# Three reorderings in a two-layer decoder step: merged tiles rounded one by one, the first pair of a normalised stage, and gated splits behind masks

## What is computed

```python
h = rmsnorm(x, norm1_g) * (1.0 + sc1) + sh1
z = h @ w_in                                   # q | k | v | g | xl | gl | ma | mb, 8192 columns
q = rope(q); k = rope(k) * DK_RET ** -0.5
o, s_ret_new = retention(q, k, v, s_ret)       # per-head decay, chunks of 128; then a norm per head
p_ret = (o * silu(g)) @ w_proj_ret
p_lru = rg_lru_block(xl, gl, ...) @ w_proj_lru
m = sigmoid(ma) * p_ret + sigmoid(mb) * p_lru
x = x + gt1 * (m @ w_out)
h2 = rmsnorm(x, norm2_g) * (1.0 + sc2) + sh2
x = x + gt2 * (square(relu(h2 @ w_mlp1)) @ w_mlp2)
```

## Time and profile before

| | |
|---|---|
| median of 3 runs | 2120.17 us (2119.0 to 2121.91) |
| the profiled execution, its own time | 2128.43 us |
| its span, first to last instruction | 2126.6 us |
| mean granted clock of TensorE | 0.988 |
| PE busy | 2071.5 us, 97% |
| DVE, ACT, POOL busy | 50%, 34%, 11% |
| DMA | 232.68 MB, mean 109 GB/s |

### The profile page before, as it was taken

How to read it: one execution, slowest core, us unless ns; L and a number is a source line. 1 busy time by engine, 2 the same in 40 slices (tenths; PEclk the granted TensorE clock), 3 DMA queues, 4 the chain that set the end, 5 groups by cost and what they waited for, 6 DMA issues and landing times.

```text
span 2126.6 us, 36627 instructions
## 1 busy us (share of the span) xinstructions
PE 2071.5 (97%) x15244; PEld 1985.4 (93%) x15244; DVE 1072.9 (50%) x1691; ACT 726.6 (34%) x931; POOL 231.8 (11%) x238
## 2 busy tenths in 40 slices
PE   6999999999999999999999999999999999999997
PEld 3899989999998999999989998899999899999997
DVE  4535556675345444444455355667734453535353
ACT  3124434665233222222231244446632321212122
POOL 0001020000032000000220011100000410101014
PEclk8999999999999999999999999999999999999998
DMA  8542243222243333333332313422222422222222
GB/s 344 188 147 86 76 159 99 80 77 82 87 151 109 119 114 120 114 120 119 119 139 80 99 56 125 139 85 78 78 90 71 157 70 82 88 80 81 87 81 100
DMA packets 78924, 232.68 MB, mean 109 GB/s; under 512 B 7360, under 2 KB 27840, under 8 KB 78528
## 3 DMA queue, kind: packets, MB, share of 16 engines
q1 hardware_dynamic: 56304, 204.86, 28.1%
q10 hardware_dynamic: 22480, 25.78, 3.8%
HBM read 218.52 MB, written 12.09 MB: 108 GB/s over the span
## 4 chain that ended last, share of the span: by engine, by line
PE 96%; DVE 2%; DMA 1%; ACT 1%; issue 1%; SPq 0%; DVEq 0%
PE acc L1205 85%; PE acc L1256 2%; PE misc L1277 2%; PE misc L1437 1%; DMA first_raw<-ada_in 1%; PE misc L1398 1%; PE misc L1371 1%; PE misc L1374 1%; PE misc L1373 0%; PE acc L1262 0%; PE misc L1391 0%; DVE qk L755 0%; PE misc L1330 0%; PE misc L1286 0%; PE misc L1347 0%
## 5 line engine op out<-in xcount | busy, mean ns | idle before, releaser
L388 ACT ACTIVATE weight_h<-raw 128x1024 fp32r<-128x1024 f32 x288 | 305.0, 1059 | 1054.0 <-PE acc L1205 1009.3
L1205 PE MATMUL acc<-h_hi,weight_h 128*128 128x288 f32 x2688 | 585.3, 299 | 7.3 <-DVE o_t L823 5.2
L1205 PE MATMUL acc<-h_hi,weight_l 128*128 128x288 f32 x2688 | 576.6, 296 | 0.0
L1205 PE MATMUL acc<-h_lo,weight_h 128*128 128x288 f32 x2688 | 575.9, 296 | 0.0
L744 DVE TENSOR_TENSOR weight_l<-raw,weight_h 128x1024 fp32r<-128x1024 f32 x288 | 398.5, 1384 | 266.2 <-ACT weight_h L388 266.2
L1205 PEld LDWEIGHTS acc<-h_hi,weight_h 128*128 128x128 f32 x2688 | 434.2, 189 | 20.9 <-issue 16.0
L1205 PEld LDWEIGHTS acc<-h_hi,weight_l 128*128 128x128 f32 x2688 | 433.7, 189 | 0.0
L1205 PEld LDWEIGHTS acc<-h_lo,weight_h 128*128 128x128 f32 x2688 | 433.7, 189 | 0.0
L1205 PE MATMUL acc<-b_hi,weight_h 128*128 128x288 f32 x1792 | 385.9, 297 | 4.8 <-DVE b_lo L1024 4.8
L1205 PE MATMUL acc<-b_hi,weight_l 128*128 128x288 f32 x1792 | 384.9, 297 | 0.0
L1205 PE MATMUL acc<-b_lo,weight_h 128*128 128x288 f32 x1536 | 329.9, 297 | 0.0
(11 more groups left out here) (203 smaller groups left out, 1662.5 us busy)
## 6 DMA issues: line engine op xcount, KB each, us to landing
raw<-stream SPq DMA_DIRECT2D x290, 512.0 KB, 3.5
ada_raw<-ada_in SPq DMA_DIRECT2D x72, 512.0 KB, 5.6
s_s<-state_in ACTq DMA_DIRECT2D x8, 1024.0 KB, 5.5
ret_s_out<-s_s ACTq DMA_DIRECT2D x8, 1024.0 KB, 4.4
first_raw<-ada_in SPq DMA_DIRECT2D x12, 512.0 KB, 19.3
two_raw<-ada_in SPq DMA_DIRECT2D x12, 512.0 KB, 10.4
x<-x_in ACTq DMA_DIRECT2D x1, 2304.0 KB, 13.8
wrg<-wrg_in ACTq DMA_DIRECT2D x18, 128.0 KB, 2.9
```

What stands on the lines that cost most here:

```text
L388: A(weight_h[:, j % 2, :], raw[:, (j + 2) % 4, :], ACT.Copy).then_inc(h_split, 1)
L1205: last = M(acc[j % 2][:, half, 0:HALF], w, r[:, k, half * HALF:(half + 1) * HALF], start=(k == 0 and n == 0), stop=(k == KT - 1 and n == 2))
```

## The change

Four edits. (1) In AT_LRU each merged part is rounded and split inside its own tile, into `h_hi` and `h_lo`, whose last reader is AT_MB, and AT_OUT reads these. (2) In `first_pair` the products with `h_lo` of tile 0 stand ahead of the second half of the high products of tile 1. (3) In Q and K the weight split stands behind the three rotary instructions. (4) In AT_G the gated parts 0 and 1 are split at tile 4, and 2 and 3 at tile 6, each time behind the masks; parts 4 and 5 stay at tile 7.

```diff
--- ACT
-                plain(lay, AT_LRU, 1)
-                zero = lay * 0
-                for j in range(3):
-                    split_h(lay, AT_LRU + 4, zero, j)
-                act.wait_ge(tile_done, lay * LAYER_TILES + (AT_LRU + 8))
                 for m in range(KT):
+                    split_h(lay, AT_LRU, 0, m)
                     act.wait_ge(m_ready, lay * 8 + m + 1)
-                    A(one(b_hi, zero + m), one(mix, zero + m), ACT.Copy).then_inc(m_rounded, 1)
-                split_h(lay, AT_LRU + 4, zero, 3)
+                    A(one(h_hi, m), one(mix, m), ACT.Copy).then_inc(m_rounded, 1)
--- DVE, Q and K
-                        split_l(lay, off, 0, j)
                         done(lay, off, 0, j)
...
                         V.scalar_tensor_tensor(t2[64:128], a[0:64], factor, sin[0:64], ALU.mult, ALU.mult).then_inc(acc_free, 1)
+                        split_l(lay, off, 0, j)
                         copied(lay, off, 0, j)
--- DVE, AT_G
                             V.tensor_tensor(kd_s[0:NB_S], kt, km, ALU.mult).then_inc(s_masked_ready, 1)
+                            if m > 3:
+                                split_gated(m - 4)
+                                split_gated(m - 3)
...
-                        if j % 2 and m > 1:
-                            split_gated(m - 3)
-                            split_gated(m - 2)
+                        if m == 7:
+                            split_gated(4)
+                            split_gated(5)
--- DVE, AT_LRU
-                with dve.Fori(0, 1) as i:
-                    for j in range(4):
-                        merge(i, j)
-                        split_l(lay, AT_LRU, i, j)
...
                 for m in range(KT):
-                    split_merged(m)
-                split_l(lay, AT_LRU + 4, zero, 3)
+                    merge(m)
+                    if m:
+                        split_merged(m - 1)
+                    split_l(lay, AT_LRU, 0, m)
+                split_merged(KT - 1)
--- PE
+                on_high(0, 0)
+                on_high(0, KT // 2)
+                on_high(1, 0)
+                on_low(0)
+                on_high(1, KT // 2)
+                on_low(1)
...
-                plain(lay, AT_OUT, b_hi, b_lo, b_parts(m_split, lay * 8))
+                plain(lay, AT_OUT, h_hi, h_lo, b_parts(m_split, lay * 8))
```

More of the change, by code:

```diff
@@ L1023, in split_merged @@
                     dve.wait_ge(m_rounded, lay * 8 + m + 1)
-                    V.tensor_tensor(one(b_lo, zero + m), one(mix, zero + m), one(b_hi, zero + m).bitcast(F32), ALU.subtract).then_inc(m_split, 1)
-                with dve.Fori(0, 1) as i:
-                    for j in range(4):
-                        merge(i, j)
-                        split_l(lay, AT_LRU, i, j)
-                zero = lay * 0
-                for j in range(4):
-                    merge(zero + 1, j)
-                    if j < 3:
-                        split_l(lay, AT_LRU + 4, zero, j)
-                for m in range(KT):
-                    split_merged(m)
-                split_l(lay, AT_LRU + 4, zero, 3)
+                    V.tensor_tensor(one(h_lo, m), one(mix, m), one(h_hi, m).bitcast(F32), ALU.subtract).then_inc(m_split, 1)
+                for m in range(KT):
+                    merge(m)
[3 more added lines that the diff above has]
+                split_merged(KT - 1)
                 def gated_add(j, m, gate_at, base, signal, left):
@@ L1249, in first_pair, with on_high @@
                 pe.wait_ge(acc_free, lay * LAYER_TILES + off + 2)
-                for j in range(2):
-                    for k in range(KT):
+                def on_high(j, first):
+                    for k in range(first, first + KT // 2):
                         if j == 0:
```

14 lines of the change are left out of this document (5 added, 9 removed).

## The result

The changed kernel has a median of 2104.32 us (4 runs, 2103.36 to 2105.45). The kernel before, run beside it, has 2121.04 us (4 runs, 2119.0 to 2128.86). The ratio is 0.9907 with a 95% interval of 0.9881 to 0.9934: 0.8 to 0.9% faster (the ratios here are those on record; the quotient of the medians is 0.9921), as forecast in sign. In size the medians differ by 16.7 us where 22.3 were forecast. The time itself lies 6.4 us above the forecast of 2097.9 and 1 us above the upper end of its range.

What follows compares the result with a forecast made beforehand. PE, busy for 97% of the span, was taken as the bound. Merge 8.3, pairs 10.1 and masks 3.9 sum to 22.3 us off the median of 2120.17: 2097.9 us, range 2095.0 to 2103.3.

Steps and rivals of the forecast that it cites:

- merge: AT_LRU and AT_OUT: rounding tile by tile removes 2.40 us of gap and 1.77 of clock per layer, 8.3 us.
- first pairs and rotary: First pairs of Q and MLP: 5.2 us of gaps, 3.3 clock, 2.1 MLP waits, less 0.5 new wait: 10.1 us.
- masks: AT_G: masks ahead of the gated splits remove four waits of 0.98 us before the sample output, 3.9 us.
- part 7: Last merged part, wanted by PE 5.6 us after it goes on, ready after 4.2: 1.2 us to spare.
- no tile is slow behind a gap of 1.0 us: MLP of layer 0: two tiles behind the short gap take 12.75 us, so such gaps were said to cost no clock.
- The lower bound given for this term: First pairs: 5.5 us, with no clock, 0.5 us of wait in three more places and 0.4 of split left over.
- The new wait of 0.5 us for `h_lo` in layer 1's Q pair: Tile 0's low half starts 2.13 us sooner, so PE waits 0.5 us for VectorE's eighth subtraction.
- the rival of the late state DMA: AT_G: the sample output waits for the state's DMA, so the masks edit gives nothing: 2101.8 us, chance 0.06.
- the pairs' own waits grow: All four first pairs wait for low parts, the split comes late, one clock stretch lost: 2100.7 to 2102.4 us, chance 0.09.
- the projection stage starves: AT_LRU: tile-by-tile rounding delays the weight split PE needs next; at 4.5 us delay 2126.7 us, slower, chance 0.02.
- The rival in which the clock comes back only in part: Behind the old gaps up to 6.8 us of clock gain is missing: 2099.6 to 2104.7 us, chance 0.13.
- I take the same microseconds off each.: The sum's 22.3 us comes off both the profiled span of 2126.6 and the runs' median of 2120.17 us.

Runs made afterwards that it cites:

- edit alone: The kernel before with one part of the change: merge 2118.27 us (ratio 0.9963), first pairs with rotary order 2116.52 (0.9960), or masks 2122.62 (0.9982).
- its neighbours with a short wait: Changed kernel, low half of tile 0 behind six of tile 1's eight high parts: in all first pairs 2098.68 us, in the MLP's alone 2105.73.

## Why the prediction was right in the trace and short in the median

**Step by step.** By the starts of the same pieces in both traces, for the two layers:

| term | forecast | trace, before to after | edit alone, upper group to upper group |
|---|---|---|---|
| merge | 8.3 | 4.2 + 4.1 | 8.9 |
| first pairs and rotary | 10.1 | 5.0 + 0.9 + 3.3 + 1.3 | 11.7 |
| masks | 3.9 | 2.0 + 2.1 | 5.0 |
| all | 22.3 | 23.0, 0.1 elsewhere | 22.8 for the changed kernel |

The single edits add up to 25.6, 2.8 more than the change as a whole. The upper groups scatter by 0.7 to 1.6 us each, and start-up alone moved by up to 1.3 us between profiled executions, so I don't read more into that.

**The merge** went as worked out: gap and slow stretch in both layers, with part 7 in time. Of the 1.77 us that the prediction calls clock, 0.24 are the restart. And its sentence that no tile is slow behind a gap of 1.0 us misread the 12.75 us: the 0.27 of the restart was hidden by the faster pace. In layer 1's MLP, at the slow pace, the wait gave 1.3 us and not 1.0.

**The first pairs.** Both gaps and both clock terms came back. (The lower bound given for this term adds up to 4.9 and not 5.5; the range does not use it.) The new wait of 0.5 us for `h_lo` in layer 1's Q pair is not there in the profiled execution. Timeline of the changed kernel there, and the granted clock (window, PE busy, PEclk, DMA share, GB/s):

```profile
1089.96 5.38 DVE L761 SCALAR_TENSOR_TENSOR h_lo<-tmp,ada,h_hi 128x512 fp32r<-128x512 f32 x8
...
1093.96 2.29 PE L1252 MATMUL acc<-h_lo,weight_h 128*128 128x288 f32 x16
```
```profile
1086.07:1089.40 3.33, 3.33 (x14) 0.52 0.00 0
```

The low products take their plain 2.29 us. PE had started the pair at the lower clock level, which in the trace before it had not, and that pushed its low half back by more than the half microsecond. So the pair lost to the clock what it was to lose to VectorE, and a little more: layer 1's Q pair gave 3.3 us instead of 3.7. The sum holds nothing for this, and it is large: from their first to their last matmul the 96 matmuls of a first pair take 13.3 to 15.5 us in the 14 profiled executions, with none to 24 of them starting 0.24 us apart, at the lower clock. Layer 0's Q pair took 14.93 us before (18 such steps) and 14.27 in the changed kernel (13), and about 0.6 of the 5.0 us come from there; layer 1's took 13.29 (none) and 14.16 (11). Where the pair starts at full clock, the forecast wait shows. The run with the old order in the MLP's pair has the same Q pair, with 1.00 from 1086 on:

```profile
1090.12 5.38 DVE L761 SCALAR_TENSOR_TENSOR h_lo<-tmp,ada,h_hi 128x512 fp32r<-128x512 f32 x8
1093.27 2.82 PE L1252 MATMUL acc<-h_lo,weight_h 128*128 128x288 f32 x16
```

2.82 instead of 2.29 us: 0.53, against 0.5 forecast.

**The masks** were ready 2.4 us before PE came, the rival of the late state DMA is out, and so are the rivals in which the pairs' own waits grow and in which the projection stage starves. The rival in which the clock comes back only in part is out for the profiled execution, but its doubt about the kernel before was sound: two of eight gaps of 2.40 us, in three of its variants and itself, cost no clock. At 1.5 us a gap and one in four, that is under 1 us in the mean and does not explain the missing 5.6.

**What failed** is one sentence of the sum: "I take the same microseconds off each." The profiled execution and the median of the runs were not of one kind. The profiled one (2128.43) had the slow pace in layer 1's MLP, the upper group. The three timed ones (2119.0 to 2121.91) lie where the lower group does; they have no trace, so their pace is inferred from their times. The 8 us between them was on the table and I passed over it as a constant offset of 0.4%. A saving may be carried from one execution to another only if both are limited by the same things. Here the change takes away the wait on which the faster pace seems to hang. From the profiled execution the sum gives 2106.1 for every execution; 15 timed ones have a median of 2105.45. From the lower group it gives 2097, where the changed kernel has no execution at all, and its neighbours with a short wait have theirs (2096.65 to 2099.92).

So, against the kernel before in its upper group, about seven of ten executions, the gain is 22.8 us, and against its lower group 13.4. That the trace's total came within 0.7 us of the forecast is in part luck: the clock at the start of the two Q pairs gave one 0.66 us and took 0.87 from the other, which nearly cancel. The wait of 1 us ahead of layer 1's MLP cost 1.3 us and was, as far as the runs show, a ticket for 10 in three executions of ten.

## What to carry to other kernels

Before you take a saving off a median, find out why the profiled execution and the median differ; if the times of one kernel fall into groups, compare group with group, and look in the traces for the stage in which they part. Moving half of a tile's work behind the point at which its consumers are signalled hides their latency at no cost: count the work left behind the signal against the consumer's chain (here 4.07 against 3.7 us) and check which operand now comes sooner than it is made. A gap on the engine that bounds is worth itself, the restart, and the clock behind it, if it is long: here 0.26 us more at any length, no clock at up to 1.4 us, and 1.3 to 1.5 us of clock behind 12 of 14 gaps of 2.4 to 2.7.

## What the hardware showed that I had not expected

- TensorE streams the same 288-column matmuls, each with its own weight load, at one of two paces with the granted clock at 1.00 throughout: 397.07 or 387.17 us for 2976 of them (0.1334 and 0.1300 us each). The slower one has three steps of 0.131 us and a fourth of 0.140. The faster one began at restarts from a wait, three times where the granted clock rose, and once at the border of two tiles without either; by their times it came in layer 1's MLP in 33 of 107 executions with a wait ahead of the stretch and in 2 of 44 without.
- The clock behind an idle time: 1.00 in all restarts behind 0.34 to 1.37 us, 0.76 over the next 7 us behind two of three waits of 1.92 us, 0.76 to 0.80 behind three of three of 2.71 us; behind two of eight gaps of 2.40 us 1.00, behind the other six and six of 2.58 to 2.67 us 0.76 to 0.78.
- A restart costs 0.26 us beyond the listed wait: 397.07 against 396.81 us for 2976 matmuls at the slower pace.
- A low clock at the start of a pair can hide a wait inside it: 3.33 us at 0.52 took the place of 0.53 us of waiting for `h_lo`.
